# A boundary by whole rows behind the first mixer, and the roots of eight attention heads from split squares

## The chip, the cores and the metric

The kernel runs on one core of one Trainium2 chip. The metric is the device time of one execution in microseconds (us). The engines are named as the profile names them: PE is TensorE's matmul, PEld its weight load, DVE is VectorE, ACT is ScalarE, POOL is GpSimd, SP is SyncE, whose queue issues most of the loads.

## The reference, cut to what matters

Two transformer blocks follow each other on a sequence of 512 tokens of width 1024. The first block is feed-forward, mixer, feed-forward; the second is a mixer and a feed-forward. The mixer of the first block adds two branches, a state-space branch and a differential attention of eight heads:

```
out = rmsnorm(out, subln_g) * (1.0 - lam_init)        # each of the 8 heads, over its 128 values
...
merged = gates[:, :, 0] * y_ssd + gates[:, :, 1] * y_att
h = h + rmsnorm(merged @ w_out, mix_post_g)
h = h + 0.5 * rmsnorm(swiglu(rmsnorm(h, ffn2_pre_g), w_gate, w_up, w_down), ffn2_post_g)
```

with `rmsnorm(x, g) = x / sqrt(mean(x*x) + eps) * g`. The change touches two places: the root of each attention head's norm, and all that lies between the last product of `merged @ w_out` and the first products of the second feed-forward network (`ffn2`).

## The kernel before, in words

**Layout.** Activations lie transposed: 128 channels on the partitions, the 512 tokens along the free side. The running sum `hT` is 8 such blocks, k = 0 to 7 (`KB = 8`). A product with a weight panel (1024 input channels by 128 output channels) is made in float32 accuracy from three products in the reduced float type fp32r: each operand is split into a high part and a low part, and `mm` (L2198 to L2211) does high by high, high by low and low by high for each of the 8 blocks, 24 matmuls of 512 columns per panel, into one PSUM bank. The weight split is a cast on ACT (L2586) and a subtraction on DVE (L2943), into one of `NHL = 3` buffers `hl`; a buffer can be filled again when the matmuls of its last panel are done. The normed input is split into `uR` (high in slot 0, low in slot 1). The sum of squares over the channels is a matmul with a constant matrix `onesc`, in plain float32 (`rstd`, L2274 to L2282), which is followed on ACT by Ln and Exp to give the root.

**Order of the work.** A planner in Python writes out a list of steps, and each engine's program then runs its own part of every step in that list's order; waits are on semaphores. In the two mixers the function `schedule` (from L1183) interleaves a main stream (projections, panel by panel, given out two blocks at a time) with side streams (the state-space core, the attention heads), and uses the cost table (`costs`, L135, and `COSTS`, L181) to decide when a side step may be put: `ready` holds a side step until the planner's own clock of PE has passed the moment at which its inputs are estimated to be there. The numbers of that table change nothing on the chip but this order. Attention heads run in pairs (`att_side`); head h+4 is projected in the main stream only after the output of head h is planned (`chained`).

**A head's norm** (`att_head`, `side_rstd`). The head's output `o` is squared on ACT, the squares are summed by one float32 matmul of 512 columns in `rstd`, then Ln and Exp on ACT, and the scaled output is split into two pages for the later product with `wda`.

**The boundary behind the first mixer.** The eight panels of `w_out` are products with the merged pages `mR`. After each of the first seven ACT squares the result from its bank, and scales it with the gain to a page `y` (`collect`), and DVE adds the squares into one page. The last panel is done in two halves of 256 columns (tokens) by `last_rows`: half 0, with two float32 sums of the seven panels' squares in between (`end_first`, L2242), then half 1, with the second sum of half 0 in its middle (`end_sum`, L2247) and that of half 1 behind it. So the root of half 0 is ready while half 1 is still multiplied. `boundary` then goes on by halves: `post_h` (DVE, two blocks of 256 columns in one instruction: L2982 the product with the root, L2991 the addition to `hT`), `post_hi` (ACT, L2642, the high part of `uR`), `post_lo` (DVE, L2997, the low part), and `lead` (PE, L2258, L2259, L2261), which starts the first three panels of `ffn2` on what is ready, half 0 of all three panels first and then half 1. In the second half ACT also squares `hT`, and DVE adds these squares in a tree (`sq_sum`, L3008). The fourth panel follows with whole rows through `mm`; half way in it the float32 sum of the tree gives the root of `ffn2`'s own norm, by which all four results are scaled. `boundary` is used three times in the kernel; the call behind the first mixer is the second of them.

**Pages and banks.** PSUM has 3 main banks (`MB`) and 5 side banks (`SB`). `raw` holds 4 weight slots of 1024 columns and 4 more slots of 512 columns (`T1`, `T3`, `T2`, `T4S`), which only the feed-forward networks use, for sums of weight blocks that DMAs and DVE form (`sum_by_dma`, `tsum_2`, `tsum_4`).

Of the kernel before, what the change touches and what calls it, by code (L numbers as in the profile page):

```python
# [15 lines left out]
KB = 8  # L16
# [118 lines left out]
def costs(s):  # L135

    k, w = s["kind"], s.get("i", 0) + 1
    if k == "mm":
        return [("PE", 0.68 * len(s["xs"]), "pe_gemm.mm")]
    if k == "split":  # L140
        return [("ACT", 1.0, "act_split.hi"), ("DVE", 1.2, "dve_split.lo")]
    if k == "fold":
        n = len(s["ks"])
        return [("ACT", 0.65 * n), ("DVE", 0.67 * n, "dve_norm.lo", s["ks"][-1])]
    if k == "lead":
        return [("PE", 0.36 * sum(len(ks) for i, half, ks in s["units"]), "pe_gemm.mm", 2)]
# [44 lines left out]
    "norm_u": [("ACT", 0.6), ("DVE", 5.0, "dve_norm.lo", 7)],   # L191
# [62 lines left out]
def build(nc, d, out):  # L254
# [17 lines left out]
    raw = sb(ctx, "raw", [128, 2 * NRAW + 4, 512])  # L272
# [7 lines left out]
    fp = Pages(low, "fA")  # L280
    home = {id(b): (fA, i) for i, b in enumerate(low)}
# [288 lines left out]

    def side_rstd(src, which):
# [110 lines left out]
    def half_root(T, half, ready):  # L682
        s = step("end_sum", b=T["sum"][half], q=T["q"], ready=ready, r=T["r"], cols=halves[half])
        T["sum"][half].release(("act_end.ln", s))
        return [("act_end.r", s)], ("pe_end.sum", s)

# [194 lines left out]
    def ffn(wg, wu, wd, gpost, gpre, n, free, n0):  # L881
# [38 lines left out]
        def load_pair(j):  # L920
            if j < FB:
                loads["next"] += loads["next"] % 2
                r1, t1 = load(wg[j], KB * 128)
                r2, t2 = load(wu[j][:, 512:1024], 512, 1)
                rs[j] = 2 * r1, t1, 2 * r2, t2
                t3 = T1 + j % 2
                ts[j] = {T1: sum_by_dma(2 * r2, f"t1_{r2}", wu[j][:, 0:512], wg[j][:, 0:512], list(loads["free"][r2])),
                         T3: sum_by_dma(t3, f"t3_{j % 2}", wu[j][:, 0:512], wu[j][:, 512:1024], list(t3_free[j % 2]))}

        def second_sum(j):  # L930
            if j < FB:
                ts[j][T2] = step("tsum_2", b1=rs[j][0], t3=T1 + j % 2, landed=[rs[j][1], ts[j][T3]])

        def fourth_sum(j):
            if j < FB:
                ts[j][T4S] = step("tsum_4", b1=rs[j][0], s=ts[j][T2])
# [322 lines left out]
    rp.left = [(b, t_phase) for b, _ in rp.left]  # L1259
    boundary(T, [WIN[j] for j in (80, 0, 1, 2, 3, 32)], True,  # L1260
# [311 lines left out]
    def att_head(h):  # L1572
# [31 lines left out]
        r = yield from side_rstd([(o[:, :], o.t)], O128)  # L1604
# [68 lines left out]
    P = pairs_of(mg)  # L1673
    for m in range(KB - 1):
        b = MB.take()
        j = panel(d["wout"][m], KB * 128)
        b.t = [mm(j, b, P, True, True)]
        collect(ys, b, "mix_post")
    T, t_out = last_rows(ys, [(d["wout"][KB - 1], P)], "mix_post", False, "ffn2_pre")
    for hi, lo, tk in mg:  # L1680
        hi.release(*t_out)
        lo.release(*t_out)
# [508 lines left out]
    def tensor_program(e):  # L2191
# [56 lines left out]

        def lead(s):
# [24 lines left out]
        def rstd(s):  # L2274
# [6 lines left out]
            t.then_inc(*sig("pe_norm.sum", s))  # L2281

# [256 lines left out]
        do = {"mm": mm, "product": product, "lead": lead, "keep": keep, "mm_half": mm_half, "end_first": end_first, "end_sum": end_sum, "rstd": rstd, "decay_turn": decay_turn, "ssd_x": ssd_x, "ssd_cb": ssd_cb,  # L2539
# [10 lines left out]
    def scalar_program(e):  # L2550
# [82 lines left out]

        def last_sq(s):
            after(*s.bt, *s.q.after)
            activate(s.q[:, s.cols], s.b[:, s.cols], ACT.Square).then_inc(*sig("act_col.sq", s))

# [251 lines left out]
        def sp_front(s):  # L2889
# [7 lines left out]
              "con": con_load, "split": split, "fold": fold, "fold_sq": fold_sq, "end_add": end_add, "end_sum": end_sum, "squares": squares, "rstd": rstd, "warm": warm,  # L2897
              "last_sq": last_sq, "post_hi": post_hi, "norm_u": norm_u, "fold_h": fold_h, "ffn_gate": ffn_gate, "ffn_mul": ffn_hi, "collect": collect,
# [10 lines left out]
    def vector_program(e):  # L2909
# [64 lines left out]

        def post_h(s):
# [7 lines left out]
            else:  # L2983
# [8 lines left out]
                                   in1=hT[:, k:k + 2, s.cols], op0=ALU.mult, op1=ALU.add).then_inc(*sig("dve_post.h", s))  # L2992

# [582 lines left out]
        def merge2(s):  # L3576
# [8 lines left out]
              "tsum_2": tsum_2, "tsum_4": tsum_4, "fast_add": fast_add, "fast_mul": fast_mul, "split": split, "scale": scale, "fold": fold, "fold_sq": fold_sq, "end_add": end_add, "end_out": end_out, "post_h": post_h, "post_lo": post_lo, "sq_sum": sq_sum,  # L3585
# [187 lines left out]
```

## Time and profile before

| What | Value |
|---|---|
| Median of 3 runs | 2519.91 us (2519.55 to 2521.11) |
| The profiled execution, its own time | 2520.09 us |
| Its span, first to last instruction | 2518.3 us |
| PE busy | 2481.8 us, 99% of the span |
| DVE busy | 1619.7 us, 64% |
| ACT busy | 1205.7 us, 48% |
| Granted TensorE clock, mean | 0.997 of full speed |
| Chain that ended last | PE 92%, DVE 5%, DMA 2%, ACT 1% |

The profile is of one execution. A busy PE means that some matmul was in flight, and neighbouring matmuls overlap: the time that one costs in a stream is the distance from its start to the start of the next, not its recorded duration. In a timeline the columns are start, duration (both us), engine, line, operation, output and inputs, partitions by elements, and the count; in brackets stands the idle time of the engine ahead of it and who ended it.

### The profile page before, as it was taken

The page shows a single profiled execution, that of the slowest core. Times are in us where ns is not written, and L with a number is a line of the kernel's source. Part 1 is how long each engine was busy: PE and PEld are TensorE (multiplying, and loading weights), DVE is VectorE, ACT ScalarE, POOL GpSimd, SP SyncE. Part 2 cuts the span into 40 slices and gives each one's busy share as a digit, 9 for nine tenths or more (in the row PEclk, how much of TensorE's full clock was granted, in tenths as well). Part 3 has the DMA queues.
Part 4 walks back from the last instruction along what each step waited for, and adds up shares of the span by engine and source line. Part 5 has one row for each costly group of instructions (what it writes and reads, how often), then busy time and mean ns, then how long its engine had stood idle before and what let it go on. Part 6 is the DMA issues. An engine that isn't in the chain of part 4 may idle for free.

```text
span 2518.3 us, 37877 instructions
## 1 busy us (share of the span) xinstructions
PE 2481.8 (99%) x15440; PEld 2070.1 (82%) x15440; DVE 1619.7 (64%) x2585; ACT 1205.7 (48%) x2030; POOL 75.2 (3%) x114
## 2 busy tenths in 40 slices
PE   9999999999999999999999999999999999999998
PEld 7999888888877777878999888777776788888887
DVE  6888348866764554357887257766877655677733
ACT  6556244666555455245555246544333454444421
POOL 0111000000000000000110000000000000000000
PEclk9999999999999999999999999999999999999999
DMA  5776332222222222333775323211111112333232
GB/s 173 175 179 154 108 100 92 77 76 75 84 68 68 76 66 77 91 92 101 176 177 151 98 93 101 76 41 37 44 43 52 59 55 88 94 99 101 88 100 72
DMA packets 80525, 237.82 MB, mean 94 GB/s; under 512 B 8928, under 2 KB 10976, under 8 KB 80352
## 3 DMA queue, kind: packets, MB, share of 16 engines
q1 hardware_dynamic: 68832, 213.56, 27.0%
q0 software_dynamic: 10080, 18.35, 4.8%
q10 hardware_dynamic: 1440, 3.49, 0.4%
q8 instruction: 122, 2.00, 0.3%
q14 instruction: 51, 0.42, 0.1%
HBM read 233.27 MB, written 2.10 MB: 93 GB/s over the span
## 4 chain that ended last, share of the span: by engine, by line
PE 92%; DVE 5%; DMA 2%; ACT 1%; issue 1%; SPq 0%; ACTq 0%; DVEq 0%
PE bank L2208 22%; PE bank L2210 21%; PE bank L2209 21%; PE bank L2222 4%; PE bank L2224 4%; PE bank L2223 4%; PE bank L2441 2%; PE bank L2366 1%; PE bank L2280 1%; PE bank L2374 1%; DMA raw<-in_w2u 1%; PE bank L2360 1%; PE bank L2537 1%; PE bank L2347 1%; PE bank L2258 1%
## 5 line engine op out<-in xcount | busy, mean ns | idle before, releaser
L2208 PE MATMUL bank<-uR,hl 128*128 128x512 f32 x1684 | 685.4, 407 | 5.3 <-DVE uR L2954 2.8
L2943 DVE TENSOR_TENSOR hl<-raw,hl 128x1024 fp32r<-128x1024 f32 (+2 forms) x325 | 386.0, 1191 | 453.9 <-ACT hl L2586 452.8
L2210 PE MATMUL bank<-uR,hl 128*128 128x512 f32 x1684 | 658.3, 391 | 0.0
L2209 PE MATMUL bank<-uR,hl 128*128 128x512 f32 x1684 | 657.7, 391 | 0.0
L2586 ACT CAST hl<-raw 128x1024 fp32r<-128x1024 f32 (+2 forms) x325 | 329.8, 1020 | 207.2 <-PE bank L2210 196.1
L2208 PEld LDWEIGHTS bank<-uR,hl 128*128 128x128 f32 x1684 | 316.8, 188 | 94.8 <-issue 24.8
L2209 PEld LDWEIGHTS bank<-uR,hl 128*128 128x128 f32 x1684 | 317.1, 188 | 67.6 <-issue 7.2
L2210 PEld LDWEIGHTS bank<-uR,hl 128*128 128x128 f32 x1684 | 316.5, 188 | 67.7
L2937 DVE TENSOR_TENSOR hl<-raw,hl 128x1024 fp32r<-128x1024 f32 (+1 forms) x142 | 150.8, 1076 | 32.4 <-ACT hl L2582 29.4
L2222 PE MATMUL bank<-sum,hl 128*128 128x256 f32 x560 | 159.3, 284 | 2.5 <-DVE fA L3082 2.5
L2223 PE MATMUL bank<-sum,hl 128*128 128x256 f32 x560 | 158.7, 283 | 0.0
L2224 PE MATMUL bank<-sum,hl 128*128 128x256 f32 x560 | 158.7, 283 | 0.0
L2582 ACT CAST hl<-raw 128x1024 fp32r<-128x1024 f32 (+1 forms) x142 | 130.8, 925 | 53.7 <-PE bank L2224 34.4
L2208 PE MATMUL bank<-mR,hl 128*128 128x512 f32 x312 | 124.3, 398 | 0.0
L2210 PE MATMUL bank<-mR,hl 128*128 128x512 f32 x312 | 122.9, 394 | 0.0
L2209 PE MATMUL bank<-mR,hl 128*128 128x512 f32 x312 | 122.8, 394 | 0.0
L2563 ACT ACTIVATE fA<-fA 128x512 f32<-128x512 f32 (+2 forms) x107 | 65.4, 618 | 118.3 <-DVE fA L3047 61.5
L2222 PE MATMUL bank<-uR,hl 128*128 128x256 f32 x420 | 119.2, 284 | 1.1 <-ACT fA L2563 1.1
L2223 PE MATMUL bank<-uR,hl 128*128 128x256 f32 x420 | 119.1, 284 | 0.0
L2224 PE MATMUL bank<-uR,hl 128*128 128x256 f32 x420 | 119.1, 283 | 0.0
L2222 PEld LDWEIGHTS bank<-sum,hl 128*128 128x128 f32 x560 | 107.5, 192 | 3.8 <-issue 3.6
L2223 PEld LDWEIGHTS bank<-sum,hl 128*128 128x128 f32 x560 | 107.6, 192 | 0.1
(499 smaller groups left out, 4385.5 us busy)
## 6 DMA issues: line engine op xcount, KB each, us to landing
raw<-in_win SPq DMA_DIRECT2D x147, 512.0 KB, 3.5
raw<-in_w SPq DMA_DIRECT2D x44, 512.0 KB, 3.5
raw<-in_w1u SPq DMA_DIRECT2D x54, 256.0 KB, 3.0
raw<-in_w2u SPq DMA_DIRECT2D x51, 256.0 KB, 3.1
raw<-in_w1g SPq DMA_DIRECT2D x22, 512.0 KB, 4.5
raw<-in_w2g SPq DMA_DIRECT2D x22, 512.0 KB, 4.3
raw<-in_w1d SPq DMA_DIRECT2D x16, 512.0 KB, 3.6
raw<-in_wssd SPq DMA_DIRECT2D x16, 512.0 KB, 3.5
```

The costliest lines, as they stand in the source:

```text
L2208: e.matmul(s.bank[:, :], h[:, 0, w], hi, start=s.first and q == 0, stop=False)
L2209: e.matmul(s.bank[:, :], h[:, 0, w], lo, start=False, stop=False)
L2210: i = e.matmul(s.bank[:, :], h[:, 1, w], hi, start=False, stop=s.last and q == n - 1)
L2222: e.matmul(to, h[:, 0, w], hi, start=s.first and k == 0, stop=False, skip_group_check=True)
L2223: e.matmul(to, h[:, 0, w], lo, start=False, stop=False, skip_group_check=True)
L2224: i = e.matmul(to, h[:, 1, w], hi, start=False, stop=k == 3, skip_group_check=True)
L2441: i = e.matmul(b[r, at], x[r, at], y[r, at], start=True, stop=True)
L2563: return e.activation(o, i, func, **k)
L2582: e.copy(hi, x).then_inc(*sig("act_split.hi", s))
L2586: e.copy(hl[j % NHL][:, 0, w], rawslot(s.r)[:, w]).then_inc(*sig("act_split.hi", s, i))
L2937: e.tensor_tensor(lo, x, hi.bitcast(F), ALU.subtract).then_inc(*sig("dve_split.lo", s))
L2943: e.tensor_tensor(h[:, 1, w], x[:, w], h[:, 0, w].bitcast(F), ALU.subtract).then_inc(*sig("dve_split.lo", s, i))
```

## The change

**Heads.** The sum of squares of the eight attention heads is no longer a float32 matmul. ACT copies the squares into a high part in fp32r, DVE subtracts it from the squares to get the low part, and PE makes two fp32r matmuls with `onesc` read as fp32r. The two parts lie in 4 new pages `sqR`, on the memory of the four 512-column slots at the end of `raw`; so the sums of weight blocks in the second feed-forward network now also wait until these pages are free. The cost table has entries for the new steps (0.47 of PE in place of 0.9; 0.62 of ACT and 0.69 of DVE for the split).

**Boundary behind the first mixer.** It has a function of its own, `boundary_whole`. The last panel of `w_out` is multiplied in whole rows, with the float32 sum of the seven panels' squares after its fourth block. After the last block come the squares of the last panel (ACT), their sum and the root, three dummy products (`keep(3)`), and then `post_fold`: block by block of 512 columns, DVE multiplies by the root, adds to `hT` and makes the low part, and ACT makes the high part and squares. `lead_all` multiplies the three first panels block by block, 9 matmuls of 512 columns per block. What follows (the tree, the fourth panel, the root, the scaling) is as before. The other two boundaries keep the halves.

```diff
+    if k == "rstd_split":
+        return [("PE", 0.47, "pe_norm.sum"), ("ACT Ln", 0.7, "act_norm.ln"), ("ACT Exp", 0.63, "act_norm.r")]
+    if k == "sq_split":
+        return [("ACT", 0.62), ("DVE", 0.69, "dve_norm.sq_lo")]
...
-    raw = sb(ctx, "raw", [128, 2 * NRAW + 4, 512])
+    with ExitStack() as ph:
+        raw = sb(ph, "raw", [128, 2 * NRAW + 4, 512])
+    sb(ctx, "raw_slots", [128, 2 * NRAW, 512])
+    sqR = sb(ctx, "sqR", [128, 4, 512], R)
...
+    def rstd_split(x, which):
+        yield from ready(x)
+        q = fp.take()
+        s = step("squares", src=[(x[:, :], list(x.t))], qs=[q])
+        yield from until(lambda: len(sp.left) > 1)
+        hi, lo = sp.take(), sp.take()
+        s = step("sq_split", q=q, hi=hi, lo=lo, ready=[("act_norm.sq", s, 0)])
+        q.release(("dve_norm.sq_lo", s))
+        yield from ready(("dve_norm.sq_lo", s), banks=1)
+        b, r = SB.take(), fp.take()
+        r.s = s = step("rstd_split", hi=hi, lo=lo, of=s, which=which, b=b, r=r)
...
+    def boundary_whole(ys, b7, b_sum, gpost, half, gpre, srcs, normed, drop=None, con=None):
+        q = fp.take()
+        s = step("last_sq", b=b7, bt=list(b7.t), q=q, cols=slice(0, 512))
+        js = [panel(srcs[0], KB * 128)]
+        r = rstd([(q[:, :], [("act_col.sq", s)])], O1024, b_sum)
+        q.release(("pe_norm.sum", r.s))
+        keep(3)
...
+        s = step("post_fold", ys=ys, b=b7, r=r, gpost=gpost, half=half, gpre=gpre, h=[list(t) for t in t_h],
+                 hr=[list(t) for t in t_hr], last=list(u_last), qs=qs)
...
+        js += [panel(src, KB * 128, False) for src in srcs[1:3]]
...
+        s = step("lead_all", js=js, bs=bs, s=s)
...
-                         T3: sum_by_dma(t3, f"t3_{j % 2}", wu[j][:, 0:512], wu[j][:, 512:1024], list(t3_free[j % 2]))}
+                         T3: sum_by_dma(t3, f"t3_{j % 2}", wu[j][:, 0:512], wu[j][:, 512:1024], free + t3_free[j % 2])}
...
-                ts[j][T2] = step("tsum_2", b1=rs[j][0], t3=T1 + j % 2, landed=[rs[j][1], ts[j][T3]])
+                ts[j][T2] = step("tsum_2", b1=rs[j][0], t3=T1 + j % 2, landed=[rs[j][1], ts[j][T3], *free])
...
-        r = yield from side_rstd([(o[:, :], o.t)], O128)
+        r = yield from rstd_split(o, O128)
...
-    for m in range(KB - 1):
+    for m in range(KB):
         b = MB.take()
         j = panel(d["wout"][m], KB * 128)
-        b.t = [mm(j, b, P, True, True)]
-        collect(ys, b, "mix_post")
-    T, t_out = last_rows(ys, [(d["wout"][KB - 1], P)], "mix_post", False, "ffn2_pre")
+        P = pairs_of(mg)
+        if m < KB - 1:
+            b.t = [mm(j, b, P, True, True)]
+            collect(ys, b, "mix_post")
+        else:
+            mm(j, b, P[:4], True, False)
+            b_sum = sum_first(ys[0].acc)
+            b.t = [mm(j, b, P[4:], False, True, off=4)]
...
-    boundary(T, [G2[0], U2[0], G2[1], U2[1]], False,
+    boundary_whole(ys, b, b_sum, "mix_post", False, "ffn2_pre", [G2[0], U2[0], G2[1], U2[1]], False,
              drop=lambda: t_all.extend(drop_pages(NB1, rp, 1)))
-    ys, tail = ffn(G2, U2, d["w2d"], "ffn2_post", "ffn2_pre", 2, t_all, FIRST2)
+    t_sq = [x for _, after in sp.left for x in after]
+    ys, tail = ffn(G2, U2, d["w2d"], "ffn2_post", "ffn2_pre", 2, t_all + t_sq, FIRST2)
...
+        def lead_all(s):
+            for i in range(3):
+                go.wait_ge(*on("dve_split.lo", splits[s.js[i]]))
+                after(*s.bs[i].after)
+            hs = [hl[j % NHL] for j in s.js]
+            for k in range(KB):
+                w = slice(k * 128, (k + 1) * 128)
+                go.wait_ge(*on("act_norm.hi", s.s, k))
+                if k < KB - 1:
+                    for b, h in zip(s.bs, hs):
+                        e.matmul(b[:, :], h[:, 0, w], uR[:, 0, k, :], start=k == 0, stop=False)
+                    for b, h in zip(s.bs, hs):
+                        e.matmul(b[:, :], h[:, 1, w], uR[:, 0, k, :], start=False, stop=False)
+                    go.wait_ge(*on("dve_norm.lo", s.s, k))
+                    for b, h in zip(s.bs, hs):
+                        e.matmul(b[:, :], h[:, 0, w], uR[:, 1, k, :], start=False, stop=False)
...
+        def rstd_split(s):
...
+            one = onesc[:, s.which, :].bitcast(R)
+            e.matmul(s.b[:, :], one, s.hi[:, :], start=True, stop=False)
+            e.matmul(s.b[:, :], one, s.lo[:, :], start=False, stop=True).then_inc(*sig("pe_norm.sum", s))
...
+        def post_fold(s):                                   # ACT
+            after(*s.last)
+            for k in range(KB):
+                go.wait_ge(*on("dve_post.h", s, k))
+                e.mul(uR[:, 0, k, :], hT[:, k, :], pc(s.gpre, k)).then_inc(*sig("act_norm.hi", s, k))
+                after(*s.qs[k].after)
+                activate(s.qs[k][:, :], hT[:, k, :], ACT.Square).then_inc(*sig("act_norm.sq", s, k))
...
+        def post_fold(s):                                   # DVE
...
+            mul(0)
+            add(0)
+            mul(1)
+            lo(0)
+            add(1)
+            for k in range(2, KB):
+                mul(k)
+                add(k)
+                lo(k - 1)
+            lo(KB - 1)
...
         def tsum_4(s):
             go.wait_ge(*on("dve_fast.t", s.s))
+            after(*s.after)
```

In `lead_all` the last block (k = 7) is done panel by panel, three matmuls each, the last of which signals that panel's end.

## Rows read from the trace of the kernel before

**Rows 1.** The page's first part: busy time of TensorE over the whole span

```profile
PE 2481.8 (99%) x15440; PEld 2070.1 (82%) x15440; DVE 1619.7 (64%) x2585; ACT 1205.7 (48%) x2030; POOL 75.2 (3%) x114
```

**Rows 2.** Busy time by stretch: mixer, then boundary (PE, PEld, DVE, ACT, POOL, granted clock)

```profile
600.00:1119.00 519.00, 519.00 (x2506) 409.16 (x2505) 276.95 (x490) 262.10 (x516) 5.11 (x14) 1.00 0.25 78
1119.13:1150.04 30.91, 26.50 (x201) 24.78 (x199) 22.64 (x42) 18.07 (x37) 0.00 (x0) 1.00 0.14 49
```

**Rows 3.** Timeline of TensorE around the sum of one attention head's squares

```profile
771.59 1.02 PE L2280 MATMUL bank<-fB,onesc 128*128 128x512 f32 x2
...
772.67 0.39 PE L2209 MATMUL bank<-uR,hl 128*128 128x512 f32 x1
772.90 0.40 PE L2210 MATMUL bank<-uR,hl 128*128 128x512 f32 x1
```

**Rows 4.** Timeline of VectorE: the last head's output is ready

```profile
992.26 0.69 DVE L3245 TENSOR_TENSOR mR<-fA,mR 128x512 fp32r<-128x512 f32 x1
```

**Rows 5.** Timeline of TensorE: the first product that reads the heads' outputs

```profile
1018.65 0.40 PE L2208 MATMUL bank<-mR,hl 128*128 128x512 f32 x1
```

**Rows 6.** Timeline of TensorE, boundary behind the first mixer

```profile
1119.13 0.29 PE L2235 MATMUL bank<-mR,hl 128*128 128x256 f32 x1
...
1127.02 0.70 PE L2247 MATMUL bank<-fA,onesc 128*128 128x256 f32 x2 [0.47 <-ACT fA L2563]
...
1134.81 0.38 PE L2261 MATMUL bank<-uR,hl 128*128 128x256 f32 x1 [1.65 <-DVE uR L2997]
...
1135.66 0.28 PE L2261 MATMUL bank<-uR,hl 128*128 128x256 f32 x1
...
1148.25 0.28 PE L2261 MATMUL bank<-uR,hl 128*128 128x256 f32 x1
...
1150.04 0.50 PE L2208 MATMUL bank<-uR,hl 128*128 128x512 f32 x1 [0.79 <-DVE hl L2943]
1150.38 0.40 PE L2209 MATMUL bank<-uR,hl 128*128 128x512 f32 x1
...
1152.67 0.39 PE L2210 MATMUL bank<-uR,hl 128*128 128x512 f32 x1
1153.27 1.10 PE L2280 MATMUL bank<-fA,onesc 128*128 128x512 f32 x2 [0.21 <-DVE fA L3008]
```

**Rows 7.** Timeline of ScalarE, boundary behind the first mixer

```profile
1119.33 0.60 ACT L2563 ACTIVATE fA<-bank 128x512 f32<-128x512 f32 x1 [3.46 <-PE bank L2210]
...
1120.39 1.04 ACT L2586 CAST hl<-raw 128x1024 fp32r<-128x1024 f32 x1
...
1126.58 0.38 ACT L2563 ACTIVATE fA<-bank 128x256 f32<-128x256 f32 x1 [0.51 <-PE bank L2237]
...
1148.57 3.04 ACT L2586 CAST hl<-raw 128x512 fp32r<-128x512 f32 x4 [3.62 <-PE bank L2261]
```

**Rows 8.** Timeline of VectorE, boundary behind the first mixer

```profile
1121.54 1.23 DVE L2943 TENSOR_TENSOR hl<-raw,hl 128x1024 fp32r<-128x1024 f32 x1 [0.89 <-ACT hl L2586]
...
1127.44 0.68 DVE L2982 TENSOR_TENSOR fB<-fB 128x512 f32<-128x512 f32 x1
1128.16 0.69 DVE L2991 SCALAR_TENSOR_TENSOR hT<-fB,hT 128x512 f32<-128x512 f32 x1
1128.77 0.88 DVE L2997 SCALAR_TENSOR_TENSOR uR<-hT,par,uR 128x256 fp32r<-128x256 f32 x2
...
1149.30 1.29 DVE L2943 TENSOR_TENSOR hl<-raw,hl 128x512 fp32r<-128x512 f32 x2 [2.94 <-ACT hl L2586]
...
1155.84 2.48 DVE L2947 TENSOR_TENSOR fA<-bank,fA 128x512 f32<-128x512 f32 x4 [0.45 <-ACT fA L2563]
```

**Rows 9.** Timelines of the kernel's start: high and low parts of whole rows

```profile
11.13 0.72 ACT L2592 ACTIVATE uR<-hT,par 128x512 fp32r<-128x512 f32 x1 [1.05 <-DMA hT<-in_xT]
...
14.20 2.73 DVE L2954 SCALAR_TENSOR_TENSOR uR<-hT,par,uR 128x512 fp32r<-128x512 f32 x4
```

**Rows 10.** Timeline of SyncE's queue: the second network's first sums of weight blocks

```profile
1171.05 1.38 SPq L2177 DMA_DIRECT2D raw<-in_w2u  x2
```

More of the change, by code:

```diff
@@ L190 @@
     "scale": [("DVE", 0.62, "dve_norm.scaled")], "norm_x": [("DVE", 5.4, "dve_norm.x", 7)],
-    "norm_u": [("ACT", 0.6), ("DVE", 5.0, "dve_norm.lo", 7)],
+    "norm_u": [("ACT", 0.6), ("DVE", 5.0, "dve_norm.lo", 7)], "lead_all": [("PE", 17.0, "pe_gemm.mm", 2)],
     "half_ev": [("ACT", 0.6, "act_ev.out")], "qkv_ev": [("ACT", 0.6, "act_ev.out")],
@@ L280, in build @@
     fp = Pages(low, "fA")
+    sp = Pages([], "square pages")
     home = {id(b): (fA, i) for i, b in enumerate(low)}
@@ L569, in rstd @@
         return r
+    def rstd_split(x, which):
[9 more added lines that the diff above has]
+        r.s = s = step("rstd_split", hi=hi, lo=lo, of=s, which=which, b=b, r=r)
+        b.release(("act_norm.ln", s))
+        for x in (hi, lo):
+            x.release(("pe_norm.sum", s))
+        r.t = [("act_norm.r", s)]
+        return r
     def side_rstd(src, which):
@@ L685, in half_root, with sum_first @@
         return [("act_end.r", s)], ("pe_end.sum", s)
+    def sum_first(c):
+        b = SB.take()
+        s = step("sum_first", c=c, b=b)
+        c.release(("pe_norm.first", s))
+        return b
+    def boundary_whole(ys, b7, b_sum, gpost, half, gpre, srcs, normed, drop=None, con=None):
[5 more added lines that the diff above has]
+        keep(3)
+        if con is not None:
+            con()
+        ys.append(twos[1])
+        qs = [fp.take_of(low)] + [fp.take() for _ in range(KB - 1)]
+        s = step("post_fold", ys=ys, b=b7, r=r, gpost=gpost, half=half, gpre=gpre, h=[list(t) for t in t_h],
+                 hr=[list(t) for t in t_hr], last=list(u_last), qs=qs)
+        for k in range(KB):
+            t_h[k] = [("dve_post.h", s, k)]
+            t_u[k] = [("dve_norm.lo", s, k)]
+            t_hr[k] = [("dve_norm.lo", s, k), ("act_norm.sq", s, k)]
+            ys[k].release(*t_h[k])
+        b7.release(("dve_post.y", s, KB - 1))
+        r.release(("dve_post.y", s, KB - 1))
+        js += [panel(src, KB * 128, False) for src in srcs[1:3]]
+        for part in range(2):
+            s2 = step("sq_sum", need=("act_norm.sq", s, 5 if part == 0 else 7), qs=qs, part=part, before=s2 if part else None)
+            for k in ((1, 3, 5), (7, 2, 6, 4))[part]:
+                qs[k].release(("dve_norm.tree", s2, k))
+            open_split(js[0] + NHL + part, 2 - part)
+        acc = qs[0]
+        acc.t = [("dve_norm.tree", s2, 4)]
+        bs = [MB.take(), MB.take(), SB.take()]
+        s = step("lead_all", js=js, bs=bs, s=s)
+        for i in range(3):
+            ends[js[i]] = s, i
+            bs[i].t = [("pe_gemm.mm", s, i)]
+        for n, src in enumerate(srcs[3:]):
+            j = panel(src, KB * 128)
+            b = (SB, SB, MB)[n].take()
+            for q in range(0, KB, STEP):
+                if n == 0 and q == KB // 2:
+                    r = late["r"] = rstd([(acc[:, :], acc.t)], O1024, r=fp.take_of(low))
+                    acc.release(("pe_norm.sum", r.s))
+                b.t = [mm(j, b, [u_at(k) for k in range(q, q + STEP)], q == 0, q + STEP == KB, off=q)]
+                last = [] if q == 0 else last
+                last += b.t * STEP
+            if n == 0:
+                if drop:
+                    drop()
+                for i in range(3):
+                    ahead[id(srcs[i])] = scaled(bs[i], r)
+                if normed:
+                    xs = [fp.take() for _ in range(KB)]
+                    s_x = step("norm_x", g=gpre, r=r, xs=xs, h=[list(t) for t in t_h])
+            bs.append(b)
+            if n:
+                ahead[id(srcs[n + 2])] = scaled(bs[n + 2], r)
+        u_last[:] = b.t
+        if normed:
+            s = step("norm_u", xs=xs, s=s_x, last=last)
+            for k in range(KB):
+                t_u[k] = [("dve_norm.lo", s, k)]
+                t_hr[k] = [("dve_norm.x", s_x, k)]
+                xs[k].release(*t_u[k])
+        ahead[id(srcs[-1])] = scaled(b, r)
+        if normed:
+            r.release(*late["t"])
+            late.clear()
@@ L1259, in build @@
     rp.left = [(b, t_phase) for b, _ in rp.left]
+    sp.left = [(sqR[:, i, :], t_phase) for i in range(4)]
     boundary(T, [WIN[j] for j in (80, 0, 1, 2, 3, 32)], True,
@@ L2632, in warm, with sq_split @@
                 table[0] = want
+        def sq_split(s):
+            after(*s.ready, *s.hi.after)
+            e.copy(s.hi[:, :], s.q[:, :]).then_inc(*sig("act_norm.sq_hi", s))
         def last_sq(s):
```

53 lines of the change are left out of this document (45 added, 8 removed).

## The prediction

> **What bounds the kernel now.** The page's first part comes first: PE is in flight for 99% of the span [rows 1]. Then the busy times by stretch, for the two stages that the change touches. From 600 to 1119 us, the mixer with all its attention heads, PE is busy for the whole 519.00 us at full granted clock, DVE for 277 and ACT for 262 [rows 2]. So each microsecond that PE no longer has to work there comes off the time, and some microseconds more on DVE and ACT cost nothing, as long as none of their results comes late. The boundary is another matter: of the 30.91 us from the first matmul of the last `w_out` panel to the first of the fourth `ffn2` panel PE is busy for 26.50, idle for 4.41 [rows 2], and the reader should look at what ends each idle time. The longest, 1.65 us, is ended by DVE's low part, 0.79 by DVE's split of a weight panel, 0.47 by ACT's squares [rows 6]. There a chain through three engines counts, not PE's work.
>
> A measured change of this kernel can be told from none from about 0.2% on, 5.0 us.
>
> **Heads.** Removed is one float32 sum per head. In its stream the sum starts at 771.59, one matmul (L2208) stands behind it, and the next starts follow at 772.67 and 772.90 [rows 3]. At 0.23 us from start to start, L2208 began at 772.44, so the sum took 0.85 us. Added are two fp32r matmuls of the same 512 columns, 2 x 0.23 = 0.46. Each head saves 0.39 us, eight heads 3.1 us. The sum alone could gain less if each change between float32 and fp32r cost a refill, about 0.1 us by 1150.04 to 1150.38 against 0.23 [rows 6]: 8 x 0.29 = 2.3 is the lower end. Upper end: if the f32 sum took four passes of 0.23, 8 x 0.46 = 3.7. I take 3.1, the stream's own value.
>
> Here a rule bears on it. Two records of 0.85 us in all stand for one float32 sum of 512 columns [rows 3]. The Trainium skill, page FP8 and Floating Point Precision, section TensorE Precision Notes, says that a true float32 product goes through the array in four passes. By that rule a head would save 0.46 us and the eight 3.7; by the record they save 3.1. The record decides, and the rule's case is a rival below.
>
> Each head also gets a copy of 512 on ACT and a subtraction on DVE, with waits between them some 1.4 us of chain; 8 x 0.6 us of ACT and 8 x 0.7 of DVE lie beside a PE that is busy all the time, on engines half idle [rows 2]. The last head's output is ready at 992.95 and first read at 1018.65 [rows 4, 5], so 25.7 us of cover stand against four pairs of heads, each later by 1.4 us and at most one planner step of 1.4 us (six matmuls): 11 us. I cost it at nothing. If that cover were gone, PE would wait for the difference. The planner's order shifts a little, since its costs change; with no PE wait in the stretch there is none to gain, only one to make. The four new pages use the memory of the weight sums' slots. The first such load of `ffn2` goes out at 1171.05 [rows 10], and the last head's sum is over before 992. The longer list of waits names nothing later than the fourth panel's root (1153.27 plus 1.10 us [rows 6]), so neither SP's queue nor DVE's sums behind it, nor POOL's adding loads, start later. Nothing.
>
> **Boundary.** I lay the new order out from the same start, 1119.13 [rows 6].
>
> PE: twelve matmuls (2.76), the float32 sum of the seven panels' squares (0.85), twelve more (2.76): 1125.5, and the last one is in flight for 0.16 more, 1125.7. Before, they ended at 1126.54, 0.04 ahead of ACT's 1126.58 [rows 7].
>
> Root: ACT starts 0.04 after PE ends (1148.25 + 0.28 to 1148.57), the square of 512 from a bank takes 0.60 [rows 7]: 1126.35. PE follows ACT by 0.06 (1126.96 to 1127.02) [rows 6, 7]: 1126.4. From the start of a float32 sum over Ln and Exp to DVE's first product it takes 1155.84 - 1153.27 = 2.57 us [rows 6, 8]: 1129.0. In between the third lead panel's split fits: its buffer is free at 1125.7, ACT's cast (1.04 [rows 7]) lies behind the square and ends at 1127.3, before Ln can start at 1127.5; DVE's part (1.23 [rows 8]) ends at 1128.6, 0.4 before it is in the way.
>
> First block: the product and, 0.72 later [rows 8], the addition, which ends at 1130.4; ACT's high part of 512 takes 0.72 [rows 9], so PE starts the lead at about 1131.2. `keep(3)` is 3 x 0.85 us of dummy work from 1127.3 to 1129.8, and hides nothing that counts; PE is idle for about 0.7 and 1.2 us around it, 1.9 in all where 4.4 were idle before.
>
> Lead: 72 matmuls. Whole rows start 0.229 apart (1150.38 to 1152.67, ten) [rows 6]; halves started 0.120 apart (1135.66 to 1148.25, 105) [rows 6], so whole rows are also 0.01 cheaper per pair. Per block PE needs 9 x 0.23 = 2.07 us; DVE needs 0.72 + 0.61 [rows 8] and 0.68 for a low part of 512 (2.73 / 4 [rows 9]), 2.01. PE sets the pace, barely. The first panel's last matmul is the 66th: it starts at 1131.2 + 0.1 + 65 x 0.23 = 1146.25 and ends at 1146.65. Before, it ended at 1148.53. ACT then splits the fourth panel (1148.57), DVE follows 0.73 later (1149.30), PE at 1150.04 [rows 6 to 8]: everything behind hangs on this, so the gain is 1.9 us. DVE must be free at 1147.4: its eighth addition ends near 1144.0, its last low part near 1145.5, three sums of the tree (0.61 each) 1147.3. It just fits; I take 1.85.
>
> Bounds: if DVE's instructions did not overlap (0.72 + 0.72 + 0.75 per block), eight blocks come 1.4 us later and 0.5 is left. Upwards DVE's tree stops it at 2.0.
>
> **Sum.** 3.1 + 1.85 = 4.95 us. The profiled execution took 2520.09 us, of which 2518.3 are its span and 1.8 lie around it, unchanged: 2515.1. It stands 0.18 above the median of 2519.91, so the forecast against the median is 2515.0.
>
> **The rivals.**
>
> DVE paces the boundary. 2.01 against 2.07 us is a thin margin, and the first two blocks run hand over hand: the second high part should be ready at the very moment PE wants it. For it: PE's longest waits before were for DVE's low parts. Against: a per-block need still under PE's. If it gives back 1 to 1.4 us, the gain is 3.6 to 4.0: about 2516.2.
>
> Four passes. The sum is counted too short by the records, and the heads save 3.7: total 5.55, 2514.4. Against: the next matmuls' starts [rows 3], which no error in an end can move.
>
> The mixer loses part of it. The planner's new order or a later eviction makes PE wait somewhere, 1 to 3 us: around 2517. Against: no idle time at all in 519 us.
>
> Slower. `chained` holds the main stream until a head's output is planned. If heads 0 to 3 were late enough, PE would have only the heads' own steps in its queue, and would pay each head's longer chain itself: 8 x 1.4 = 11.2 us, less 4.95, gives 2526. It decides from the point where a head's split stands alone on PE's path, in any of the four pairs. For it: the chain does get longer, and the hold exists. Against: it existed before too, and PE never waited for a head [rows 2].
>
> I gave the clock no case: it stayed granted at full speed through an idle time of 1.65 us [rows 2, 6], longer than any that I expect.
>
> **How the numbers follow.** Forecast 0.64, DVE's pace 0.13, four passes 0.09, loss in the mixer 0.09, slower 0.05. The forecast's own range, both bounds of the heads and 0.3 us of the boundary, is 2514.2 to 2516.2; its middle lies at the very bound of 0.2% (2514.9), so I count 0.31 of it as faster and 0.33 as same. Faster: 0.31 + 0.09 = 0.40. Same: 0.33 + 0.13 + 0.09 = 0.55. Slower: 0.05. The range for 8 in 10 takes in four passes and DVE's pace: 2513.8 to 2517.0.
>
> **What would show it.** In the new profile the boundary from the last panel's first matmul to the fourth `ffn2` panel's first should take 29.0 to 29.2 us in place of 30.91, with idle times near 0.7 (ended by ACT's squares), 1.2 (ended by ACT's first high part), 0.3 or less for low parts, and some 0.4 to 0.8 for the weight split; the DVE should reach that split with little or no idle time. Each head's pair of matmuls should take 0.46 us, and PE should still show no idle time between 600 and 1119. The last `w_out` panel should start 3.1 us earlier in the span. I would be wrong if that shift were clearly smaller or larger, if PE waited in the mixer for an eviction or for a head's low part, or if the boundary's idle times for DVE's low parts summed to over 1 us.

## The result, and the profile after

The changed kernel takes 2512.6 us (median of 8 executions, 2512.1 to 2515.3) where the kernel before takes 2519.9 (8, 2517.3 to 2521.6) in the same comparison: ratio 0.9975, 95% interval 0.9966 to 0.9984. By the 0.2% that the prediction took as the limit it is faster, which I had at 0.40, though the interval also holds smaller gains, down to 0.16%. The median lies 1.2 us below my range (2513.8 to 2517.0). Two further comparisons, e1 and e9 below, gave 0.9980 (0.9970 to 0.9989) and 0.9971 (0.9958 to 0.9983); their medians, 2514.12 and 2513.92 us, lie inside the range.

The first profiled execution of the changed kernel took 2515.27 us, with a span of 2513.4: it is the slowest of its 8. So the profile shows 4.9 us less than the profile of before, where the medians differ by 7.3. That gap is a question of its own, taken up below. First the two stages, as in [rows 2]: the mixer, then the boundary from the last `w_out` panel's first matmul to the fourth `ffn2` panel's first.

```profile
PE 2479.0 (99%) x15346; PEld 2065.3 (82%) x15346; DVE 1622.7 (65%) x2583; ACT 1209.6 (48%) x2027; POOL 75.9 (3%) x114
...
600.00:1119.00 519.00, 519.00 (x2523) 412.03 (x2522) 283.66 (x500) 269.20 (x527) 5.12 (x14) 1.00 0.24 79
1116.71:1145.65 28.94, 26.95 (x107) 19.51 (x106) 21.58 (x32) 16.40 (x26) 0.00 (x0) 1.00 0.15 52
```

(The last panel starts at 1116.71: the float32 sum behind its twelfth matmul starts at 1119.50, and these matmuls start 0.2325 apart.) PE is still busy all through the mixer, with about 7 us more on DVE and on ACT. The boundary takes 28.94 us in place of 30.91. PE's idle time there fell from 4.4 us [rows 2] to 2.0. The waits of PE in the boundary, after:

```profile
PE bank L2362 <- ACT uR L2785: 1.2, 1, 1.2
PE bank L2411 <- ACT fB L2702: 0.7, 1, 0.7
```

Both are the root's chain. The waits for DVE's low parts, the 1.65 us of [rows 6] among them, are gone. Of the 0.79 for the weight split 0.14 is left: the matmul before the fourth panel ends at 1145.51 (1145.12 + 0.39), and the panel starts at 1145.65. A head's sum, after, against [rows 3] (timeline of PE):

```profile
773.83 0.39 PE L2313 MATMUL bank<-uR,hl 128*128 128x512 f32 x1
774.06 0.39 PE L2419 MATMUL bank<-sqR,onesc 128*128 128x512 f32 x1
774.28 0.39 PE L2420 MATMUL bank<-sqR,onesc 128*128 128x512 f32 x1
774.51 0.39 PE L2311 MATMUL bank<-uR,hl 128*128 128x512 f32 x1
```

The pair takes 0.45 us where the float32 sum took 0.85.

**The whole kernel in five stages.** The loads that SP issues mark where the stages end, since each waits for a buffer that the work sets free. The table is worked out from the rows of the loads in each profile (the first network ends with the last load of `w1d`, the mixer with the first of `w2g`, the second network with the last of `w2d`) and from the first matmul of the fourth `ffn2` panel.

| Profile | Span | network 1 | mixer | boundary | network 2 | rest |
|---|---|---|---|---|---|---|
| before | 2518.3 | 328.9 | 766.0 | 55.14 | 302.76 | 1065.5 |
| changed, first profile | 2513.4 | 330.0 | 762.5 | 53.15 | 302.35 | 1065.4 |
| e1, changed | 2511.3 | 328.6 | 762.5 | 53.12 | 301.58 | 1065.5 |
| e9, changed | 2513.5 | 331.0 | 762.5 | 53.12 | 301.28 | 1065.6 |
| e12, before | 2516.0 | 328.5 | 766.0 | 55.15 | 301.85 | 1064.5 |

The mixer and the boundary repeat to 0.03 to 0.1 us. The change is worth 3.5 us in the one and 2.0 in the other, 5.5 in all, in every profile. The two networks that form sums of weight blocks by DMA do not repeat, and the rest took 1.0 us less in e12.

### The profile page after: what moved, and what is told of

It reads as the page before. It is cut to its first block, busy times and chain, and to the rows that moved or that the text cites. A ratio compares the mean times of both kernels' runs of the same rounds, so it can differ in the third digit from the quotient of the medians.

```text
span 2513.4 us, 37708 instructions
## 1 busy us (share of the span) xinstructions
PE 2479.0 (99%) x15346; PEld 2065.3 (82%) x15346; DVE 1622.7 (65%) x2583; ACT 1209.6 (48%) x2027; POOL 75.9 (3%) x114
## 4 chain that ended last, share of the span: by engine, by line
PE 93%; DVE 4%; ACT 1%; DMA 1%; issue 1%; SPq 0%; ACTq 0%; DVEq 0%
PE bank L2311 22%; PE bank L2313 21%; PE bank L2312 21%; PE bank L2325 4%; PE bank L2327 4%; PE bank L2326 4%; PE bank L2580 2%; PE bank L2505 1%; PE bank L2411 1%; PE bank L2513 1%; PE bank L2499 1%; PE bank L2676 1%; PE bank L2486 1%; DVE hl L3094 1%; PE bank L2340 0%
## 5 line engine op out<-in xcount | busy, mean ns | idle before, releaser
L2311 PE MATMUL bank<-mR,hl 128*128 128x512 f32 x320 | 127.8, 399 | 0.0
L2313 PE MATMUL bank<-mR,hl 128*128 128x512 f32 x320 | 126.0, 394 | 0.0
L2312 PE MATMUL bank<-mR,hl 128*128 128x512 f32 x320 | 125.9, 393 | 0.0
```

What stands on the lines that cost most here:

```text
L2311: e.matmul(s.bank[:, :], h[:, 0, w], hi, start=s.first and q == 0, stop=False)
L2312: e.matmul(s.bank[:, :], h[:, 0, w], lo, start=False, stop=False)
L2313: i = e.matmul(s.bank[:, :], h[:, 1, w], hi, start=False, stop=s.last and q == n - 1)
```

## The experiments

**The changed kernel again, and each part alone.**

> The changed kernel once more, for a profile of an execution near its median. Its first profiled execution took 2515.27 us, the others about 2512.6. Theory A (the stages that the change touches gain 3.5 us in the mixer and 2.0 in the boundary, and the rest is how an execution happens to go in the feed-forward networks): the first network ends where it ended before (last load of its down panels at 328.9 us), the mixer is shorter by 3.5 us, the boundary by 2.0, 5.5 in all, and any further gain lies behind the boundary in a stage whose code did not change. Rival B (the heads or the order of the mixer gain more than the first profile shows): the mixer alone is shorter by 5 us or more.

Measured: 2514.12 us (10 executions), ratio 0.9980. Network 1 ends at 328.6, the mixer takes 762.5, the boundary 53.12. The loads on SP's queue (columns: count, shortest, median and longest issue in ns, first and last start in us), here and then in e12, the kernel before:

```profile
L2275 SPq DMA_DIRECT2D raw<-in_w1d x24: 327/328/328, 219.1 to 328.6; - x24
...
L2275 SPq DMA_DIRECT2D raw<-in_w2g x22: 327/328/434, 1091.1 to 1326.7; - x22
```

```profile
L2172 SPq DMA_DIRECT2D raw<-in_w1d x24: 327/328/328, 219.1 to 328.5; - x24
...
L2172 SPq DMA_DIRECT2D raw<-in_w2g x22: 327/328/429, 1094.5 to 1331.9; - x22
```

1091.1 - 328.6 = 762.5 against 1094.5 - 328.5 = 766.0. Rival B is out: the mixer holds 3.5 us, not 5.

```diff
-    boundary_whole(ys, b, b_sum, "mix_post", ...)
+    boundary(T, [G2[0], U2[0], G2[1], U2[1]], False, ...)      # e2, with last_rows ahead of it
...
-        r = yield from rstd_split(o, O128)
+        r = yield from side_rstd([(o[:, :], o.t)], O128)       # e3
```

> The heads' sums from split squares, with the old boundary by halves. If the parts add up as in the first profile: 3.5 us faster than the kernel before (ratio 0.9986), of which 3.1 are PE's work and 0.4 the new order. By the rival that the heads hold the surplus over my sum (the 2.4 us between a total of 7.3 and 4.95): 5.5 us faster (0.9978).

> The boundary by whole rows, with the heads' sums in float32 as before. If the parts add up: 2.0 us faster than the kernel before (ratio 0.9992), all of it between the last w_out panel and the fourth panel of the second network. By the rival that the whole-row boundary also helps what follows it: 4 us or more (0.9984), with the surplus between the fourth panel and the end of the second network.

Measured (e2, then e3): heads only 2515.59 us, ratio 0.9986 (0.9977 to 0.9995), mixer 762.5, boundary 55.29; boundary only 2516.99 us, ratio 0.9991 (0.9982 to 1.0000), mixer 766.0, boundary 53.11. The parts add up stage by stage, and neither touches the other's. e3's profiled execution took 2519.82 us, 2.8 above its median, and its second network 304.99 us, the longest seen. PE's longest waits there, and DVE's for the sums that DMAs bring, first in e3 and then in e1:

```profile
PE bank L2325 <- DVE fA L3272: 2.7, 3, 2.0
...
DVE raw L3263 <- DMA raw<-in_w2u: 11.0, 10, 3.6
```

```profile
PE bank L2325 <- DVE fA L3272: 0.9, 2, 0.6
...
DVE raw L3263 <- DMA raw<-in_w2u: 9.5, 14, 1.5
```

DVE waits up to 3.6 us for one such sum to land (1.5 in e1), and PE then stands 2.0 us in one piece. All of PE's waits in that network sum to 3.3 us in e3 and 1.5 in e1, which is 1.8 of the 3.4 us between the two. The rest lies behind the long wait, where the granted clock fell:

```profile
1335.00:1340.00 5.00, 5.00 (x37) 5.00 (x36) 4.34 (x7) 2.47 (x4) 0.00 (x0) 0.80 0.65 129
```

The number behind POOL's is the clock. From 1333.55 to 1336.95 sixteen matmuls of 256 columns start 0.21 us apart in place of 0.12, about 1.5 us more.

**The planner's costs.** The entries for the split changed nothing but the order:

```diff
     if k == "rstd_split":
-        return [("PE", 0.47, "pe_norm.sum"), ...]
+        return [("PE", 0.9, "pe_norm.sum"), ...]
     if k == "sq_split":
-        return [("ACT", 0.62), ("DVE", 0.69, "dve_norm.sq_lo")]
+        return [("DVE", 0.0, "dve_norm.sq_lo")]
```

> The changed kernel with the planner told the old costs (0.9 for a head's sum, nothing for the split), so that the order of the mixer is nearly that of the kernel before and PE's work that of the changed one. If the mixer's gain is PE's work alone: the mixer is shorter than before by 3.1 us, and this kernel equals the changed one within 0.5 us. If the new order is worth something by itself, this kernel loses that: 1 to 2 us slower than the changed one. If the old order is now too early for the split, PE waits in the mixer for DVE, which it did not before.

Measured: 2521.54 us, ratio 1.0006 (0.9997 to 1.0015); mixer 769.7, 7.2 us longer than the changed kernel's and 3.7 longer than that of before. PE's waits in the mixer and one of them in the timeline:

```profile
PE bank L2419 <- DVE sqR L3181: 4.7, 5, 1.2
...
PE bank L2419 <- ACT fB L2939: 0.6, 1, 0.6
```

```profile
772.08 0.40 PE L2313 MATMUL bank<-uR,hl 128*128 128x512 f32 x1
773.36 0.50 PE L2419 MATMUL bank<-sqR,onesc 128*128 128x512 f32 x1 [0.88 <-DVE sqR L3181]
773.69 0.40 PE L2420 MATMUL bank<-sqR,onesc 128*128 128x512 f32 x1
```

The sum is now put into PE's queue before DVE's part of the split is done, and everything behind it stands. The reader should see what such a wait really costs: from 772.08 to 773.36 are 1.28 us where 0.23 would do, and the next start comes 0.33 later in place of 0.23, so 1.15 us for a recorded idle time of 0.88. Six waits, 5.3 us recorded plus 6 x 0.27, make 6.9 of the 7.2; counted from the starts around each of the six, it is 6.92 too. With 0.9 for the sum but the split's true costs the planner writes the very same order as the changed kernel's, for every engine: the entry that carries the gain is the split's.

**Order or work.** To separate the new order from PE's shorter sums, the sums were made float32 in the changed order:

```diff
-            e.matmul(s.b[:, :], one, s.hi[:, :], start=True, stop=False)
-            e.matmul(s.b[:, :], one, s.lo[:, :], start=False, stop=True)...
+            e.matmul(s.b[:, :], onesc[:, s.which, :], s.q[:, :], start=True, stop=True)...
```

> The changed kernel in its own order, splits made as there, but each head's sum is one float32 matmul of the squares again; so the high and low parts are made and not read. Read from the last load of the first network's down panels to the first load of the second network's panels, a stretch that took 766.0 us in the kernel before and 762.5 in the changed one. If PE's work is worth my 3.1 us and the new order 0.4: 765.6. If all 3.5 is PE's work: 766.0. If the order holds most of it: 763 to 764.

Measured:

```profile
L2276 SPq DMA_DIRECT2D raw<-in_w1d x24: 327/328/328, 219.8 to 329.0; - x24
L2276 SPq DMA_DIRECT2D raw<-in_w2g x22: 327/328/433, 1094.9 to 1329.7; - x22
```

1094.9 - 329.0 = 765.9 us. So 3.4 us is PE's work and 0.1 the order. Per head that is 0.43, where the distances of starts around a sum give 0.40. Between the first two heads' sums the twelve other matmuls start 0.231 apart in the kernel before ((775.21 - 771.59 - 0.85) / 12), and the six in the changed kernel 0.227 ((775.87 - 774.51) / 6): the neighbours seem a little faster too. e5 confirms it in the same order of work: its first two sums start at 773.03 and 775.28, which leaves 1.40 us for the six matmuls between them, 1.36 in e1 (773.08 to 774.44). Why, no run here tells.

**The dummy products of the boundary.**

```diff
-        keep(3)        # e6 without it, e7 with keep(6)
```

> The changed kernel without the three dummy products of the boundary. If the chain over the root sets the lead's start, and the clock holds: the same boundary, 28.9 us from the last panel to the fourth, with PE idle for 3.8 us where it was idle for 1.2 behind the sum. If the clock falls in that gap, the lead's matmuls start 0.43 us apart in place of 0.23 for a while and the boundary is longer by 1 to 5 us.

> The changed kernel with six dummy products in place of three, 2.55 us more of PE's work behind the sum. If PE was idle there for 1.16 us as the profile says: the lead starts 1.4 us later, the boundary takes 30.3 us, and the idle time ended by ACT's high part is gone. If PE was not really idle: 2.5 us later.

Measured without them: the boundary column is 55.88 in place of 53.12, 2.8 us longer. PE, then the granted clock (the number behind POOL's) by stretches of 5 us:

```profile
1121.98 1.12 PE L2410 MATMUL bank<-fB,onesc 128*128 128x512 f32 x2 [0.69 <-ACT fB L2701]
1126.84 1.62 PE L2361 MATMUL bank<-uR,hl 128*128 128x512 f32 x3 [3.74 <-ACT uR L2784]
1128.26 1.48 PE L2363 MATMUL bank<-uR,hl 128*128 128x512 f32 x3
1129.54 1.48 PE L2366 MATMUL bank<-uR,hl 128*128 128x512 f32 x3
...
1133.12 0.85 PE L2366 MATMUL bank<-uR,hl 128*128 128x512 f32 x3
1133.82 0.85 PE L2361 MATMUL bank<-uR,hl 128*128 128x512 f32 x3
```

```profile
1125.00:1130.00 5.00, 3.16 (x8) 2.51 (x9) 4.75 (x9) 3.04 (x5) 0.00 (x0) 0.60 0.31 105
1130.00:1135.00 5.00, 5.00 (x18) 3.99 (x17) 4.89 (x9) 3.18 (x6) 0.00 (x0) 0.72 0.01 3
1135.00:1140.00 5.00, 5.00 (x24) 4.14 (x23) 4.93 (x8) 3.03 (x5) 0.00 (x0) 1.00 0.00 0
```

The lead starts no earlier: 4.86 us after the root's sum starts, 4.87 in e1. But PE, idle for 0.69 and then 3.74 us, comes back at the lower of its two levels: three matmuls take 1.28 us (1128.26 to 1129.54), and 0.70 later on. In this execution `keep(3)` would have been worth 2.8 us. It is the only one without the dummy products, so whether the clock falls in each such execution is not shown. In none of the nine profiles with dummy products did it fall in this boundary.

Measured with six: the boundary column is 54.31, 1.2 us longer, and the wait for ACT's high part is gone. First e1, then e7:

```profile
1127.42 0.93 PE L2362 MATMUL bank<-uR,hl 128*128 128x512 f32 x3 [1.17 <-ACT uR L2785]
```

```profile
1123.08 5.31 PE L2402 MATMUL bank<-onesc 128*128 128x512 f32 x12
1127.83 1.26 PE L2362 MATMUL bank<-uR,hl 128*128 128x512 f32 x3
```

Of the 2.55 us added 1.2 count and 1.35 were covered: the idle time was real.

**Two extensions, as candidates for a faster kernel.**

```diff
-        r = yield from side_rstd([(x[:, :], x.t)], O1)     # l2 norms of the second mixer
+        r = yield from rstd_split(x, O1)
```

> The changed kernel with the same split also for the 16 sums of squares of the second mixer's l2 norms, by the same four pages. If PE sets the pace there too: 16 x 0.39 = 6.2 us faster than the changed kernel (ratio to the kernel before 0.9954 with the changed one's own 0.9978). Rival: that mixer has PE waits on chains through DVE and ACT (some 12 us in all), and DVE and ACT carry more there; a longer chain per norm then adds waits, and the gain is 3 us or less, or turns into a loss where a PE instruction waits on a split as in the run with the old costs.

Measured: 2527.33 us, ratio 1.0034 (1.0022 to 1.0047). The stage behind the second network takes 1077.6 us in place of 1065.5, 12 us more. PE's waits of the second mixer, the first lines, and what the largest was in e1:

```profile
PE bank L2590 <- DVE gx L3592: 6.1, 3, 2.9
PE bank L2631 <- DVE fB L3635: 4.8, 5, 1.9
PE bank L2420 <- DVE sqR L3182: 3.8, 6, 0.9
```

```profile
PE bank L2580 <- ACT gx L3009: 2.6, 8, 0.7
PE bank L2589 <- DVE gx L3591: 2.0, 1, 2.0
```

All waits in that mixer sum to 29 us, 14 in e1. PE has some 6 us less to do (16 x 0.40), and waits 15 us more: for the splits themselves (3.8) and for chains of the next steps, which start later. The granted clock fell once more than in e1, between 1950 and 1970 (0.74 over 13.66 us of busy PE, an estimated 3.6 of the 12 us). There PE is 95 to 96% busy for 200 us even in the changed kernel, so its work was not all that set the pace.

> The changed kernel with the same split for the four sums of the state-space groups in the first mixer; the main stream there is held for nine free pages in place of six, since the group's chain holds its pages longer. By PE's work alone: 4 x 0.4 = 1.6 us faster than the changed kernel (mixer 760.9 us). Rival: the holding of the main stream, or a split that comes late, makes PE wait, and the mixer is as long as in the changed kernel or longer; PE waits inside the mixer would show it, and there were none.

Measured: 2536.77 us, ratio 1.0064 (1.0051 to 1.0076); mixer 784.3, 22 us longer. The waits that appear are for the state-space core's masked decays, not for a split:

```profile
PE bank L2495 <- DVE fB L3407: 7.4, 4, 2.1
PE bank L2495 <- DVE fA L3407: 7.3, 3, 2.6
```

Two things changed in this kernel, the split and the hold on nine free pages, without which the plan runs out of pages. The four groups of waits in the mixer sum to 16 us. Behind them the granted clock fell as well, to a mean of 0.71 from 480 to 485 and 0.86 from 600 to 650, where no other profile has a fall; I estimate 7 of the 22 us from the busy time at each clock. The waits point to the hold, which lets too little of the main stream stand between the core's steps; the two were not tried apart, so this says nothing on the split of these four sums alone.

**What differs between comparisons.**

> The changed kernel a third time. Theory: the mixer is 3.5 us and the boundary 2.0 us shorter in every execution, and all that differs from one execution to another lies in the two feed-forward networks that sum weight blocks by DMA, with both kernels alike. Then the stages outside them repeat to 0.1 us (762.5 and 53.1 us), and the ratio over many rounds settles at 1 - 5.5/2519.7 = 0.9978. Rival: the first comparison's 7.3 us between medians is real, and the ratio is 0.9971 again.

Measured: ratio 0.9971 (0.9958 to 0.9983), mixer 762.5, boundary 53.12, network 1 331.0, the longest seen.

```diff
-        r = yield from rstd_split(o, O128)
+        r = yield from side_rstd([(o[:, :], o.t)], O128)
...
-    boundary_whole(ys, b, b_sum, "mix_post", ...)
+    boundary(T, [G2[0], U2[0], G2[1], U2[1]], False, ...)      # e11, with last_rows ahead of it
```

In e11 the place of `sqR` and the second network's added waits stay. e12 is the kernel before, unchanged.

> The changed kernel with both parts taken back: float32 sums of the heads and the boundary by halves. What is left of the change is the place of the weight sums' four slots and the second network's added waits before its first weight sums. Theory: the same as the kernel before (mixer 766.0, boundary 55.1, ratio 1.000 within 0.0005). Rival: the measured difference over all comparisons so far (6.2 us between the means) exceeds the 5.5 us of the two stages because the second network runs a little better with the added waits; then this kernel is 0.7 us faster than the kernel before.

> The kernel before against itself, for what a comparison of two equal kernels gives and for a second profile of it. Mixer 766.0 and boundary 55.1 us again; the two networks anywhere in the ranges seen so far (328.1 to 331.0 and 300.9 to 305.0 us); ratio 1.000 within 0.0008.

Measured: waits only 0.9995 (0.9986 to 1.0004), mixer 766.0, boundary 55.12; the kernel before against itself 1.0001 (0.9992 to 1.0010), mixer 766.0, boundary 55.15. Five rounds place a ratio within 0.0009, 2.3 us (0.0013 in e9, with fewer executions). Over all fourteen profiles the first network took 328.1 to 331.0 us with the same code, and the second 300.9 to 305.0, where only the added waits differ: a spread of 2.9 and 4.1 us.

A large part of what differs is the granted clock. The two longest first networks, 331.0 (e9) and 330.0 (the first profile of the changed kernel), are the only ones in which it fell there. PE in that first profile, then in e1:

```profile
14.79 0.76 PE L2311 MATMUL bank<-uR,hl 128*128 128x512 f32 x1 [1.36 <-DVE uR L3105]
15.35 0.63 PE L2312 MATMUL bank<-uR,hl 128*128 128x512 f32 x1
15.78 0.63 PE L2313 MATMUL bank<-uR,hl 128*128 128x512 f32 x1
```

```profile
15.02 0.47 PE L2311 MATMUL bank<-uR,hl 128*128 128x512 f32 x1 [1.37 <-DVE uR L3105]
15.33 0.40 PE L2312 MATMUL bank<-uR,hl 128*128 128x512 f32 x1
15.56 0.39 PE L2313 MATMUL bank<-uR,hl 128*128 128x512 f32 x1
```

The idle time just ahead is the same (1.35 to 1.37 us in all fourteen profiles), and only one of the two comes back slow. What differs lies before it: an idle time near 9 us in the span, ended by the same line, of 1.23 us here and 1.36 in e9, and of at most 0.78 in all the others. The next seven starts take 3.12 us there and 1.70 in e1: 1.4 us, as much as lies between 330.0 and 328.6. In the rest of e12 a fall was shorter than elsewhere (mean clock 0.91 from 1860 to 1880, 0.83 in the other profile of the kernel before). The executions without a profile say the same: beside e1 the kernel before has a median of 2517.36 us at a mean clock of 0.998 (5 executions), 2519.44 at 0.997 (16), 2520.40 at 0.996 (8) and 2521.70 at 0.995 (2), about 1.4 us for each 0.001.

## Why the prediction was right or wrong

**The bound, and the shape of the gain: right.** PE's work set the mixer, the chain set the boundary. No wait appeared between 600 and 1119; the last head's output, ready at 996.1 in the first profile of the changed kernel, is first read at 1016.2, 20 us of cover where 25.7 stood before.

**The boundary, term by term: right, but for one wait.** Counted from the last panel's first matmul, I had the root's sum at 7.3 us, the lead at 12.1 and the fourth panel at 29.0 to 29.2. They came at 7.28 (1123.99), 12.14 (1128.85) and 28.94 (1145.65). The gain of 1.85 was 2.0. DVE's pace, the rival, was a step of 1.99 us per block (products at 1133.99 and 1135.98), 2.01 forecast, and PE never waited for a low part:

```profile
1133.99 0.69 DVE L3130 TENSOR_TENSOR fB<-fB 128x512 f32<-128x512 f32 x1
1134.71 0.69 DVE L3140 SCALAR_TENSOR_TENSOR hT<-fB,hT 128x512 f32<-128x512 f32 x1
1135.32 0.74 DVE L3145 SCALAR_TENSOR_TENSOR uR<-hT,par,uR 128x512 fp32r<-128x512 f32 x1
1135.98 0.68 DVE L3130 TENSOR_TENSOR fB<-fB 128x512 f32<-128x512 f32 x1
```

The fourth panel's split found DVE free, with 0.1 us to spare, as I had it (the tree's third sum from 1144.10 for 0.68, the split from 1144.90). PE's idle time ahead of that panel was 0.14 us, where I had given 0.4 to 0.8 as a sign.

**The heads: a size.** I took 0.39 us per head from the starts of four matmuls, 3.1 us in all; e5 against e1 gives 3.4. The order, costed at nothing, gave 0.1. The heads' 3.1 is the mis-sized term: the mixer gained 3.5. The sum of 4.95 should have been 5.5, and 2514.4 in place of 2515.0. The rival of four passes priced each pass at the 0.23 us of an fp32r matmul and forecast 3.7, which is not borne out: a float32 sum took 0.85 us in both kernels, not 0.93. Four passes as such are not refuted. At the lower clock level a matmul of 512 columns took 0.427 us (1.28 / 3 in e6); half of that is 0.213, and four times 0.213 is 0.85. The sign that I gave, a last `w_out` panel 3.1 us earlier in the span, was no good test: it came 2.4 us earlier (1116.71 against 1119.13), only because the first network took 1.1 us longer in that execution. The mixer has to be measured by itself.

**The step that put the result outside: the range.** "The forecast's own range, both bounds of the heads and 0.3 us of the boundary", and the range built on it, held only the bounds of the terms, and nothing for what differs between executions of one kernel. "I gave the clock no case" left out one of its causes. The runs show in its place a spread of some 5 us: the kernel before took 2516.8 to 2521.9 us beside e1, 1.4 us for each 0.001 of mean granted clock, and the networks wait for sums that DMAs bring. The three medians of the changed kernel differ by 1.5 us (2512.6, 2514.12, 2513.92), and only the first is outside the range. (The range also held slips of its own: the bounds given make 2514.1 to 2516.1, not 2514.2 to 2516.2, and the middle of the latter is 2515.2, not 2514.9, so "faster" had a little too much of the forecast's chance.)

Of the 2.4 us between forecast and result, 0.6 are the sum's. The rest is beyond what this explains for certain. The three comparisons give 0.9975, 0.9980 and 0.9971, 6.2 us in the mean against 5.5 in the stages. Each interval holds 0.9978, so chance is enough. In e9 the mean clock was 0.9961 for the kernel before and 0.9968 for the changed one, an estimated 1.0 us of that comparison's gain at 1.4 us per 0.001; whether the change itself has a part in that clock is not shown. e11 leaves room for a gain of up to 3.5 us by the added waits alone, and for a loss of 1.0. Whether there is any, stays open, and so does why the first median was the lowest: its executions have the same mean clock as those of e1 (0.9971).

**Two sentences that did not hold.** That `keep(3)` "hides nothing that counts": where the clock falls without it, as in e6, that costs 2.8 us. My argument for giving the clock no case, an idle time of 1.65 us that had done no harm, rested on one execution. In e11, with the same boundary by halves, the clock did fall there, behind idle times of 0.47, 0.50 and 0.62 us:

```profile
1130.00:1132.00 2.00, 2.00 (x11) 2.00 (x11) 1.97 (x5) 1.99 (x4) 0.00 (x0) 0.50 0.00 0
```

It cost nothing (boundary column 55.12), since the slower matmuls took the place of waits for low parts (1.5 us in place of 2.7). Of the four profiles of the boundary by halves it is the only one with a fall. And "I cost it at nothing" for the split beside a busy PE was right only with the planner's entries: the slower rival, PE paying for a head's longer chain, came true in e4, not by the hold on the main stream, but by a sum put into the queue too early. It cost 7.2 us there, and made the kernel slower than before in its mixer.

## What to carry to other kernels

A queue that runs in order must be told of every link that is added to a chain: the same instructions with an untrue cost in the planner turned a gain of 3.5 us into a loss of 3.7. Where PE is busy without a break, count its work by start distances and move the rest off it; where it waits for chains, as in the second mixer here, the same trade can lose. Split a profile into stages that repeat and stages that do not before comparing two executions: here 0.1 us could be read in the one, and a median of five rounds knew 2.3. Look at the granted clock of both in short stretches, and give a forecast's range a term for what executions of one kernel differ by.

## What was unexpected of the hardware

Idle times of 0.69 and then 3.74 us halved the granted clock for at least the next twelve matmuls (0.43 us from start to start in place of 0.23), while 0.69 and 1.16 with dummy work between them left it at full speed. Much shorter ones can be enough: near the kernel's start the clock fell behind idle times of 1.23, 0.58 and 1.36 us in the first profile of the changed kernel, and held behind 0.78, 0.58 and 1.37 in e1. A semaphore wait of PE cost its recorded idle time plus 0.25 to 0.28 us in the six waits of e4: the last matmul ahead is still in flight for 0.16 to 0.17 us beyond the usual distance, and the distance behind the wait's first matmul is 0.33 to 0.34 in place of 0.23.
